# A two-layer diffusion step on one core: moving the second half of each modulation slice behind the products of the slice in front

## The reference, cut to what matters

```python
def adaln(c, w, b):
    m = jax.nn.silu(c) @ w + b                     # w is 2048 x 6144
    shift, scale, gate = jnp.split(m, 3, axis=-1)
    return shift[:, None], scale[:, None], gate[:, None]

h = rmsnorm(x, norms[i]) * (1.0 + scale) + shift   # per column of 2048
q_a, k_a, v_a, q_b, k_b, v_b, gate = jnp.split(h @ w_in, idx, axis=-1)
...                                                # attention, gate, output product, residual
```

## Time and profile before

| | |
|---|---|
| time, median of 3 runs (lowest to highest) | 1322.89 us (1322.8 to 1322.94) |
| time of the profiled execution | 1325.11 us |
| its span | 1323.2 us |
| granted TensorE clock, mean | 0.997 |
| PE busy | 1296.5 us (98%) |
| DVE, ACT, POOL busy | 783.8 us, 515.4 us, 61.8 us |
| DMA moved | 257.80 MB, mean 195 GB/s |

### The profile page before, as it was taken

One profiled execution on the slowest core, in us unless ns is written; L12 is line 12 of the kernel. 1 busy time (PEld: TensorE's weight loads), 2 busy tenths in 40 slices (PEclk: granted clock), 3 DMA queues, 4 the chain that ended last, 5 costly groups with the idle time before them and its releaser, 6 DMA issues.

```text
span 1323.2 us, 17024 instructions
## 1 busy us (share of the span) xinstructions
PE 1296.5 (98%) x6611; PEld 1028.9 (78%) x6611; DVE 783.8 (59%) x1129; ACT 515.4 (39%) x880; POOL 61.8 (5%) x80
## 2 busy tenths in 40 slices
PE   5999999999999999999999999999999999999997
PEld 2566767778888878888887788887788888888885
DVE  3334766775767767775876476884444444454444
ACT  4223433344333333443333833333444333433333
POOL 2000100000100010000001100000000000000000
PEclk9999999999999999999999999999999999999999
DMA  9999788445666457535775565663332111216443
GB/s 379 383 393 388 253 303 297 134 146 177 240 211 217 142 179 259 195 131 197 271 271 210 191 219 192 220 219 125 112 98 65 51 62 64 65 51 244 151 155 132
DMA packets 70111, 257.80 MB, mean 195 GB/s; under 512 B 8504, under 2 KB 8632, under 8 KB 68752
## 3 DMA queue, kind: packets, MB, share of 16 engines
q1 hardware_dynamic: 64368, 235.48, 50.8%
q0 software_dynamic: 5520, 21.17, 4.9%
q10 hardware_dynamic: 144, 0.07, 0.0%
HBM read 248.76 MB, written 7.93 MB: 194 GB/s over the span
## 4 chain that ended last, share of the span: by engine, by line
PE 77%; DVE 3%; issue 1%; ACT 1%; POOL 0%; ACTq 0%; POOLq 0%; DVEq 0%
PE gemm L532 16%; PE gemm L534 16%; PE gemm L533 16%; PE attended L741 3%; PE turned L691 3%; PE gemm L504 2%; PE gemm L506 2%; PE gemm L505 2%; PE scores L988 2%; PE scores L992 1%; PE scores L727 1%; PE ada_bank L506 1%; PE ada_bank L505 1%; PE ada_bank L504 1%; DVE w_lo L1451 1%
## 5 line engine op out<-in xcount | busy, mean ns | idle before, releaser
L1451 DVE TENSOR_TENSOR w_lo<-w_raw,w_hi 128x1024 fp32r<-128x1024 f32 x242 | 299.1, 1239 | 290.7 <-ACT w_hi L1064 290.0
L532 PE MATMUL gemm<-w_hi,act_lo 128*128 128x512 f32 x1146 | 459.5, 401 | 0.5 <-DVE w_lo L1451 0.5
L534 PE MATMUL gemm<-w_hi,act_hi 128*128 128x512 f32 x1146 | 447.5, 390 | 0.0
L533 PE MATMUL gemm<-w_lo,act_hi 128*128 128x512 f32 x1146 | 446.6, 390 | 0.0
L1064 ACT ACTIVATE w_hi<-w_raw 128x1024 fp32r<-128x1024 f32 x242 | 253.7, 1056 | 304.6 <-PE gemm L534 247.6
L532 PEld LDWEIGHTS gemm<-w_hi,act_lo 128*128 128x128 f32 x1146 | 215.4, 188 | 53.2 <-issue 10.9
L534 PEld LDWEIGHTS gemm<-w_hi,act_hi 128*128 128x128 f32 x1146 | 215.1, 188 | 46.6
L533 PEld LDWEIGHTS gemm<-w_lo,act_hi 128*128 128x128 f32 x1146 | 215.6, 188 | 42.3
L1120 ACT ACTIVATE prob<-scores,nmax 128x384 f32<-128x384 f32 (+1 forms) x96 | 48.9, 510 | 101.5 <-DVE nmax L1642 95.3
L1642 DVE TENSOR_REDUCE nmax<-scores 128x1 f32<-128x384 f32 (+1 forms) x96 | 42.5, 465 | 69.3 <-PE scores L992 48.5
L1535 DVE SCALAR_TENSOR_TENSOR ada<-ada,silu_c 128x1024 f32<-128x1024 f32 x62 | 81.3, 1348 | 0.0
(11 more groups left out here) (326 smaller groups left out, 1578.0 us busy)
## 6 DMA issues: line engine op xcount, KB each, us to landing
w_raw<-in_w_all SPq DMA_DIRECT2D x245, 512.0 KB, 3.7
ada<-in_ada_all SPq DMA_DIRECT2D x160, 512.0 KB, 6.9
gate_ring<-in_ada_all SPq DMA_DIRECT2D x24, 512.0 KB, 4.3
gate_bc<-gate_scratch POOLq DMA_DIRECT2D x4, 1024.0 KB, 8.1
st<-x_scratch POOLq DMA_DIRECT2D x4, 768.0 KB, 5.2
x_scratch<-u POOLq DMA_DIRECT2D x3, 768.0 KB, 4.6
u<-in_x_sample SPq DMA_DIRECT2D x2, 1024.0 KB, 8.2
bias<-in_bias_all POOLq DMA_DIRECT2D x2, 1024.0 KB, 8.7
```

The source lines that it names most:

```text
L532: pe.matmul(bank_[:], alo, whi[:, kk], start=first, stop=False)
L533: pe.matmul(bank_[:], ahi, wlo[:, kk], start=False, stop=False)
L534: last = pe.matmul(bank_[:], ahi, whi[:, kk], start=False, stop=end)
L1451: dve.tensor_tensor(w_lo[:, r, 0:width], w_raw[:, r, 0:width], hi_slot(w)[:, 0:width].bitcast(F32), ALU.subtract).then_inc(lo_ready, 1)
```

## The change

The PE list, two copying lists, one order on DVE and one wait on POOL are changed:

- Token blocks: 12 of the 16 are turned before G(0), six more than before, some of them between visit 2 and visit 3 of slice 0 and before T(0). The rest, 12 to 15, follow G(0). ACT copies blocks 1, 3, 5, 7 and DVE blocks 0, 2, 4, 6, 8 before they go on to slice 0.
- In the loop over slices PE had B(e+1), G(e), T(e+1), A(e+2), Q(e). Now it has B(e+1), the first token tile of Q(e), T(e+1), the other two tiles of Q(e), A(e+2), G(e+1). So G(1) comes before B(2), and so on.
- DVE forms and applies the modulation of slice e+1 before the low part of w(2e+2), no longer behind it.
- POOL waits for eight modulated blocks, that is for slice 3, before it issues the constants.

```diff
-            ada_slice(0, [2, 3])
-            gather_slice(0)
+            ada_slice(0, [2])
             for k in range(3, 6):
                 turn_tokens(k)
+            ada_slice(0, [3])
+            for k in range(6, 9):
+                turn_tokens(k)
+            gather_slice(0)
+            for k in range(9, 12):
+                turn_tokens(k)
...
-                chunk_slot(W_KV + 2 * e + c, e, (M_KV, M_QA)[c], (hlo, 0), (G, QB)[c], None)
+                chunk_slot(W_KV + 2 * e + c, e, (M_KV, M_QA)[c], (hlo, 0), (G, QB)[c], None, tiles)
             ada_slice(1, [0, 1])
             first_chunks(0, 0)
-            for k in range(6, KT):
+            for k in range(12, KT):
                 turn_tokens(k)
-            ada_slice(1, [2, 3])
-            first_chunks(0, 1)
-            gather_slice(1)
-            ada_slice(2, [0, 1])
-            for e in range(1, SLICES):
+            for e in range(SLICES):
                 if e + 1 < SLICES:
                     ada_slice(e + 1, [2, 3])
-                first_chunks(e, 0)
+                first_chunks(e, 1, [0])
                 if e + 1 < SLICES:
                     gather_slice(e + 1)
+                first_chunks(e, 1, [1, 2])
                 if e + 2 < SLICES:
                     ada_slice(e + 2, [0, 1])
-                first_chunks(e, 1)
+                if e + 1 < SLICES:
+                    first_chunks(e + 1, 0)
...
             for e in range(SLICES - 1):
+                slice_modulated(e + 1)
                 split_lo(2 * e + 2)
-                slice_modulated(e + 1)
                 slice_low(e + 1)
                 split_lo(2 * e + 3)
...
-            pool.wait_ge(h_ready, KPS)
+            pool.wait_ge(h_ready, KT // 2)
```

More of the change, by code:

```diff
@@ L751, in _, with first_chunks @@
                 turn_tokens(k)
-            ada_slice(0, [2, 3])
-            gather_slice(0)
+            ada_slice(0, [2])
             for k in range(3, 6):
                 turn_tokens(k)
-            def first_chunks(e, c):
+            ada_slice(0, [3])
[4 more added lines that the diff above has]
+                turn_tokens(k)
+            def first_chunks(e, c, tiles=range(NT)):
                 if e == 0 and c == 1:
@@ L1161, in token_copies @@
                     copy(act_f[:, k, :], QB[k % len(QB)][:, 0:TOK]).then_inc(x0_free[1], 1)
-            token_copies([1])
+            token_copies([1, 3, 5, 7])
             copy_slice(0)
@@ L1167, in _ @@
             act_high(1)
-            token_copies([3, 5])
+            token_copies([9, 11])
             split_hi(1)
-            token_copies(range(7, KT, 2))
+            token_copies([13, 15])
             for e in range(SLICES - 1):
@@ L1746, in _ @@
                     .then_inc(xn_ready, 1)
-            token_copies([0, 2])
+            token_copies([0, 2, 4, 6, 8])
             def slice_modulated(e):
@@ L1765, in _ @@
             split_lo(1)
-            token_copies(range(4, KT, 2))
+            token_copies([10, 12, 14])
             for half in range(2):
```

## The result

The changed kernel took 1336.71 us (median of 4, 1335.28 to 1337.4) against 1322.91 us for the kernel before on the same chip: the ratio is 1.0101, interval [1.0084, 1.0119]. The forecast was 1326.7 us with a range of 1321.0 to 1333.0. The direction was right; the loss is 13.8 us, not 3.8, and lies outside the range.

The account below looks back on a forecast made before the run. PE's own work bounds behind 137.4 us, so only the first stretch, where PE and DMA ran nearly level, could move. Terms -1.5 - 4.4 - 1.4 + 2.5 + 1.3 + 7.3 = +3.8 took 1322.89 to 1326.7 us, range 1321.0 to 1333.0.

Parts of the forecast that it names:

- What bounds the kernel: Behind 137.4 us PE's own work bounds; only the first stretch, with PE and DMA nearly level, can move.
- the new lag: In the slice loop, G(e+1) follows A(e+2) at once and uses the weight slot landing next: +2.5 us.
- Wait: 0.5 us: PE wait in front of each G from G(1) to G(6), five counted: +2.5 us; none in front of Q.
- +1.3 for G(7): At G(7) no half slice is left between, so PE waits for low parts: +1.3 us.
- DMA has 0.96 us spare: In each slice of the new order DMA has 0.96 us spare, 4.8 in five, of which the ring stores part.
- +7.3 for their new place: Constants behind slice 3, about 68 us: 5.2 us lost by the stream plus 2.1 of its 3.7 us lateness.
- -4.4 for leaving the old one: Early slot waits at B(1), A(2), B(2) go: constants leave from 26 us on, G(1) stands between A(2) and B(2).
- The turned blocks: Before G(0), six turns move into waits, -2.3 us, against G(0) starting +0.8 later: -1.5 us.
- The clock: Rival: a long wait in front of G(4), then a half-clock stretch, adds 1.5 to 3 us; chance 0.15 with long lag.
- Costs nothing by itself: DVE's new order has no cost: the modulation no longer stands behind a weight slot that lands late.
- the lag is longer: Rival: landing takes 5.4 us, each G waits 2.0 us more; half gives +10, 1333 us; chance 0.15 with the clock.
- It all cancels: Rival: the reserve stores what it can, constants cost 4.1, sum +0.6 us, 1323.5 us; chance 0.32 within 2.65 us.

Follow-up runs that it names:

- run 2: Changed kernel with POOL waiting for 14 modulated blocks, so the constants come behind nearly the whole stream: 1332.1 us, ratio 1.0066.
- run 9: Changed kernel with each weight slot issued half a slice earlier in SP's list and POOL waiting for 14 modulated blocks: 1322.2 us, ratio 0.9991.
- run 8: Changed kernel with SP issuing each weight slot half a slice earlier, constants still behind slice 3: 1323.51 us, ratio 1.0007.
- run 10: Changed kernel with weight slots issued half a slice earlier and constants only after all 16 blocks are modulated: 1320.62 us, ratio 0.9981.
- run 3: Kernel before with only POOL's wait changed to 8 modulated blocks, constants in the middle: 1327.05 us, ratio 1.0031.
- run 4: Kernel before with only POOL's wait changed to 14 modulated blocks, constants at the end: 1323.42 us, ratio 1.0002.
- run 1: Changed kernel with POOL's wait as it was before, constants issued after slice 0: 1336.29 us, ratio 1.0106.
- run 5: Kernel before with only the token blocks turned earlier, 12 of 16 in front of G(0), and its copying lists: 1322.6 us, ratio 0.9998.
- run 7: Changed kernel with 11 and 8 small unused matmuls filling the waits in front of G(4) and Q(5): 1335.59 us, ratio 1.0096.
- run 12: Changed kernel with DVE's old order, the weight slot's low part ahead of the modulation: 1343.73 us, ratio 1.0161.

## Why the prediction was right in direction and wrong in size

**What bounds the kernel.** Right: both kernels take 1185.80 us behind Q(7), and everything happened in front of it.

**The step that failed** is the price of "the new lag": "5.4 us at least, median 8.7 ... weight slots of the same size take 3.1 at least and 3.7 in the median ... I take 3.4", and with it "Wait: 0.5 us" and, for Q, "no wait". The mechanism was the right one, down to the 3.4 us from the landing to G. Its size was not. The last slot of a group landed 3.8 us after its issue in the slice shown, and 3.6 to 6.3 us in the others away from the constants, where I had 3.4. The weight slot issued 0.4 us behind it came 1.8 us later in that slice, and 1.3 us later in most others, as I had it. In run 2, which shows the lag alone, the weight slot landed at s + 7.4, not s + 5.8, and the waits came to 11.9 us, where six times 0.5 is 3.0; 3.3 of them were in front of Q, where I had none. The cleanest price of the lag is run 2 against run 9: the constants have the same place in both, only SP's list differs, and both traces have a clock of 1.00 from 30 to 140 us. It is 1332.1 - 1322.2 = 9.9 us, where the sum had 2.5. With the constants in the middle of the stream it is 13.2 us (the changed kernel against run 8). The +1.3 for G(7) is no part of it; that wait is still there in run 8. The Trainium skill (DMA: Bandwidth & Descriptors, "Anatomy of one DMA — SWDGE (gpsimd) path") gives by estimate 3.2 us for a transfer of this size that POOL issues; no slot that SP issued in this stretch landed as fast, and the measurement decides. The range between 3.1 and 5.4 did hold most of the values, but I took the row from a part of the kernel in which DMA is half empty, 0.51. In the first four slices of run 2 the DMA share was 0.92 to 0.96, so the queue was not as short as I had supposed.

**What was missing from the sum.** In the ledger of the profiled execution, the waits at G and Q come to 12.1 us, where the terms 2.5 and 7.3 have 9.8, and half clock adds 6.0, which the sum had at nothing. The lag also repeats: a wait of PE delays the buffers that it frees, and these delay the next slots and the next weight slot by as much. The DMA share was 0.92 in the changed kernel and 1.00 in the one of run 10. I had written that "DMA has 0.96 us spare" in each slice. But time in which DMA is idle because nothing could be issued is lost, not saved up; that much is argued from the issue times, and no run tests it by itself.

**The constants.** Predicted +7.3 for their new place and -4.4 for leaving the old one. Having them in the middle of the stream instead of at its end costs 4.6 us in the new order (run 2 against the changed kernel) and 3.6 in the old one (run 3 against run 4); the trace had 5.8 at the waits, so 7.3 was too much, but of the right size. How they cost it is less clear. In the profiled executions the waits at G and Q are as long with the constants in the middle as with them late, 12.1 against 11.9 us. Of the 6.8 us between the two spans, 6.0 are the half clock behind the two longest waits. So in these two executions the constants did not add to the waits but gathered them; whether it is so in the others is not shown. The cause that I gave for the early waits was wrong: run 4 has them without constants, and the ring of seven slots makes them. The -4.4 came true all the same, by the other reason given for it, G(1) between A(2) and B(2). And the move by itself cost next to nothing, since run 1, with the constants early, is as slow.

**The turned blocks.** -1.5 predicted, -1.4 in the trace; but run 5 shows that in the old order most of it is waited away. A saving in front of a stretch bound by transfers is only worth something where the transfers keep up.

**The clock** stood among the rivals, at 1.5 to 3 us for one stretch. There were two, 2.8 and 3.2 us in the profiled execution. Run 7 shows the 5 us in one execution and not in the median, so its share of the loss stays open between 1 and 6 us. It is a consequence of the lag in any case: in run 8 the clock is 1.00 from 30 to 140 us. The Trainium skill (TensorE: Matmul & The Clock Gate, "Part 1: The HAM clock gate") has the clock fall when the engine has been idle; the rows agree in direction, since it fell at the two longest waits.

**DVE's order.** "Costs nothing by itself" was right and too modest: without it the changed kernel loses another 7 us (run 12).

**The rivals.** The case that came true is "the lag is longer", with the clock beside it, at 0.15; its own time, 1333, was still 3.7 us short. "It all cancels" rested on slot 63 hardly landing before 118.4; in run 10 it was issued at 110.3 and landed 4.9 us later, at 115.2. So a kernel in this order can end Q(7) 5.5 us earlier than before, not 0.5.

**The signs.** G(1) before 46 us held (45.21), and so did the waits in front of G, while ACT waits for `w_raw`. "4 us or more between 72 and 95 us" came as two waits of 1.9 and 3.4 us. "First matmul behind Q(7) at about 141 us" failed: 149.70. The sign for a wrong size was set at a slot landing in over 4 us: it was 3.6 to 6.3 for the last slots of a group, and 4.5 to 7.2 for the weight slots behind them, and 9.1 and 9.9 for the pair issued at 79 us, with the constants under way.

## What to carry to other kernels

When PE's order is changed so that a product follows directly on the work whose transfers were issued just ahead of its weights, the issue list has to be turned with it: here the half-slice step in SP's list was worth 10 to 13 us in the new order and cost 1.5 us in the old one. The landing time of a transfer in the critical chain should be taken from the most loaded rows near the place, not from a quiet part of the kernel. In a ring that the consumer refills, each wait delays the next issue, so a small lag per step comes again in every step, and the range has to reach further on that side.

## What the runs showed of the hardware that was not expected

- In the changed kernel the granted clock was 0.50 from 92.1 to 98.9 us and from 119.4 to 126.2, at waits of PE of 3.41 and 2.41 us, and matmuls took 0.77 us where 0.47 to 0.50 is usual for the first of a block. It also fell at waits of 2.07 us (run 4) and 2.10 us (in front of the G at 64.11 in run 12). It stayed at 1.00 behind the waits of up to 1.85 us in run 2, behind one of 2.24 us in front of the G at 65.84 in run 1, and behind one of 2.15 us in front of the G at 116.44 in run 12.
- Seventeen small transfers of 0.9 MB in all cost 3.6 to 4.6 us of the time in the middle of a stream whose reserve is thin (runs 2 to 4), 2.9 us where the weight slots run ahead (run 8 against run 10), and nothing at slice 0 of the old order, where PE waits anyway (run 4). 0.9 MB at 400 GB/s would be 2.2 us.
- Two transfers of 512 KB issued 0.4 us apart landed 1.2 to 2.6 us apart, 1.3 in most pairs (3.6 and 4.5 us from issue to landing at 101 us, 4.8 and 7.0 at 108 us).
